# In the Mamba scan, the state product moves ahead of the next group's decay matrix, and the gated norm's steps move to other places in the queues

## What is computed

```python
cb = einsum("blgn,bsgn->blsg", cc, bc)
xdt = xc * dtc[..., None]
y_diag = einsum("blsg,blsgr,bsgrp->blgrp", cb, decay, xdt)
y_off = einsum("blgn,bgrpn->blgrp", cc, state) * exp(acs)[..., None]
decay_to_end = exp(acs[:, -1:] - acs)
new_state = state * exp(acs[:, -1]) + einsum("bsgn,bsgr,bsgrp->bgrpn", bc, decay_to_end, xdt)
...
g = (y * silu(z)).reshape(b, s, SSM_GROUPS, NORM_GROUP)
g = g * rsqrt(mean(g * g, axis=-1, keepdims=True) + EPS)
g = g.reshape(b, s, D_INNER) * norm_w
return g @ w_out
```

## Time and profile before

| What | Value |
|---|---|
| Median of three runs | 1325.86 us (1325.69 to 1330.2) |
| Profiled execution, its own time | 1325.86 us |
| Its span | 1324.1 us |
| TensorE busy | 1287.5 us, 97% of the span |
| VectorE, ScalarE, GpSimd busy | 771.0, 674.5, 143.5 us |
| Mean granted clock of TensorE | 0.998 |

### The profile page before, as it was taken

The page is one execution under the profiler, slowest core; times in us unless marked ns, Lnnn a source line. Parts: engine busy times, 40 slices in busy tenths (PEclk is TensorE's granted clock), DMA queues, the critical chain, the costliest instruction groups (busy, mean ns, idle before and its releaser), DMA issues.

```text
span 1324.1 us, 18273 instructions
## 1 busy us (share of the span) xinstructions
PE 1287.5 (97%) x6912; PEld 1097.7 (83%) x6912; DVE 771.0 (58%) x924; ACT 674.5 (51%) x886; POOL 143.5 (11%) x208
## 2 busy tenths in 40 slices
PE   7999999999989999999999999899999999999997
PEld 6888889998778888888888888687888887998895
DVE  5655645778876555554555545866555544766563
ACT  6544446665774544443544435853645535443652
POOL 3000001019940000000000002610000000000000
PEclk9999999999999999999999999999999999999999
DMA  9655645543236455564655553322655563766401
GB/s 294 201 182 188 223 131 191 173 147 96 96 123 231 155 190 190 189 198 153 191 190 190 197 192 117 138 61 89 217 181 181 182 222 99 201 181 221 154 7 48
DMA packets 180045, 218.76 MB, mean 165 GB/s; under 512 B 8617, under 2 KB 132846, under 8 KB 179982
## 3 DMA queue, kind: packets, MB, share of 16 engines
q1 hardware_dynamic: 178606, 216.70, 50.2%
q10 hardware_dynamic: 1088, 1.05, 0.2%
q0 software_dynamic: 288, 0.15, 0.1%
HBM read 216.82 MB, written 1.05 MB: 165 GB/s over the span
## 4 chain that ended last, share of the span: by engine, by line
PE 86%; DVE 5%; ACT 4%; POOL 3%; issue 1%; DMA 0%; POOLq 0%; DVEq 0%; ACTq 0%; SPq 0%
PE acc L580 27%; PE acc L582 26%; PE acc L581 26%; PE tr L597 4%; DVE w_lo L1785 2%; POOL R_hi L2456 1%; ACT w_hi L1237 1%; POOL R_lo L2456 1%; PE aux L992 1%; ACT xT_hi L1250 1%; PE acc L973 1%; POOL xdt L2465 1%; POOL ys L2468 1%; DVE xT_lo L1810 0%; PE tr L854 0%
## 5 line engine op out<-in xcount | busy, mean ns | idle before, releaser
L1785 DVE TENSOR_TENSOR w_lo<-raw,w_hi 128x2048 fp32r<-128x2048 f32 (+1 forms) x196 | 442.4, 2284 | 186.3 <-ACT w_hi L1237 186.1
L1237 ACT ACTIVATE w_hi<-raw 128x2048 fp32r<-128x2048 f32 (+1 forms) x198 | 369.5, 1900 | 117.2 <-PE acc L582 116.5
L580 PE MATMUL acc<-w_hi,xT_hi 128*128 128x512 f32 (+1 forms) x914 | 362.6, 397 | 6.5 <-DVE w_lo L2368 2.9
L582 PE MATMUL acc<-w_hi,xT_lo 128*128 128x512 f32 (+1 forms) x914 | 355.4, 389 | 0.0
L581 PE MATMUL acc<-w_lo,xT_hi 128*128 128x512 f32 (+1 forms) x914 | 354.8, 388 | 0.0
L580 PEld LDWEIGHTS acc<-w_hi,xT_hi 128*128 128x128 f32 x914 | 172.1, 188 | 42.2 <-issue 3.4
L582 PEld LDWEIGHTS acc<-w_hi,xT_lo 128*128 128x128 f32 x914 | 172.0, 188 | 36.3
L581 PEld LDWEIGHTS acc<-w_lo,xT_hi 128*128 128x128 f32 x914 | 172.4, 189 | 33.3
L580 PE MATMUL acc<-w_hi,hT_hi 128*128 128x512 f32 x448 | 175.8, 392 | 0.3 <-DVE y_sb L2278 0.3
L582 PE MATMUL acc<-w_hi,hT_lo 128*128 128x512 f32 x448 | 174.5, 389 | 0.0
L581 PE MATMUL acc<-w_lo,hT_hi 128*128 128x512 f32 x448 | 174.3, 389 | 0.0
(11 more groups left out here) (292 smaller groups left out, 1145.7 us busy)
## 6 DMA issues: line engine op xcount, KB each, us to landing
raw<-in_ffn_w_down SPq DMA_DIRECT2D x88, 512.0 KB, 4.9
raw<-in_ffn_w_gate SPq DMA_DIRECT2D x87, 512.0 KB, 4.5
raw<-in_ffn_w_up SPq DMA_DIRECT2D x87, 512.0 KB, 5.5
raw<-in_ssm_w_in SPq DMA_DIRECT2D x48, 512.0 KB, 4.5
raw<-in_w_in_a SPq DMA_DIRECT2D x64, 256.0 KB, 4.1
raw<-in_ssm_w_out SPq DMA_DIRECT2D x16, 512.0 KB, 4.0
raw<-in_mla_w_out SPq DMA_DIRECT2D x8, 512.0 KB, 4.4
raw<-in_w_out_a SPq DMA_DIRECT2D x8, 512.0 KB, 4.7
```

Source lines behind the costliest of these rows:

```text
L580: pe.matmul(o, lh, rh, start=start, stop=False, skip_group_check=skip)
L582: return pe.matmul(o, ll, rh, start=False, stop=stop, skip_group_check=skip)
L1237: inst = act.activation(w_hi[:, u % RING, 0:n], raw[:, u % RING, 0:n], ACT.Copy)
L1785: inst = dve.tensor_tensor(w_lo[:, u % RING, 0:n], raw[:, u % RING, 0:n], w_hi[:, u % RING, 0:n].bitcast(F32), ALU.subtract)
```

## The change

The task `state` is gone as a task of its own. TensorE's `y` now issues the state product right behind the 16 matmuls of y, ahead of `seg`; ScalarE copies the state under `y`, ahead of the exponentials. GpSimd's `xdtd` no longer waits for the state product of the group before. The norm's steps are moved out of `small`:

| Work | Before | After |
|---|---|---|
| gate(0), (1), (2) on VectorE | in small(16), (17), (19) | behind small(16), (18), (20) |
| gate(3) | in small(21), behind its off | behind scale_gated(2) |
| scale_gated(0), (1) | in small(18), (20), behind y | behind small(18), (20) |
| scale_gated(3) | ahead of small(22) | behind the splits of O3 and O4, ahead of small(23) |
| square_gated(1), (2), (3) on ScalarE | behind the split at the end of s = 8, 9, 10 | behind first_tap of s = 9, 10, and behind the loop |
| gated_norm(0), (1), (2) on GpSimd | behind small(17), (18), (20) | behind small(17), (19), (21) |

```diff
-MAMBA_TURNS = {"dt": 1, "acs": 1, "btok": 1, "xs": TB, "cb": 1, "y": 2, "seg": 0, "state": 0, "g": TB}
+MAMBA_TURNS = {"dt": 1, "acs": 1, "btok": 1, "xs": TB, "cb": 1, "y": 2, "seg": 0, "g": TB}
...
-    for name, first in (("y", 13), ("seg", 12), ("state", 13)):
+    for name, first in (("y", 13), ("seg", 12)):
...
                             last.then_inc(turned, 1)
+                            claim_turn(k + 1)
+                            pe.wait_ge(xdtd_ready, g + 1)
+                            pe.matmul(tr[:, (k + 1) % 2, 0:GW], Btok[:, g, :], xdtd[:], start=True, stop=True)\
+                                .then_inc(turned, 1)
                             state_turn[g] = k + 1
                             c.turn += 2
-                        elif name == "state":
-                            k = state_turn[g]
-                            claim_turn(k)
-                            pe.wait_ge(xdtd_ready, g + 1)
-                            pe.matmul(tr[:, k % 2, 0:GW], Btok[:, g, :], xdtd[:], start=True, stop=True)\
-                                .then_inc(turned, 1)
...
-                        elif name == "state":
-                            act.wait_ge(turned, k)
-                            inst = act.activation(state[:], tr[:, (k - 1) % 2, 0:GW], ACT.Copy)
-                            turn_free(inst, k - 1)
+                        elif name == "y":
+                            act.wait_ge(turned, k + 2)
+                            inst = act.activation(state[:], tr[:, (k + 1) % 2, 0:GW], ACT.Copy)
+                            turn_free(inst, k + 1)
...
                     first_tap(s)
-                    if s == 8:
-                        square_gated(0)
+                    if s >= 8:
+                        square_gated(s - 8)
                     small(2 * s + 1)
                     split_to(u0 + 2 * s + 4)
-                    if s >= 8:
-                        square_gated(s - 7)
+                square_gated(3)
...
-                            if g == G + 1:
-                                gate(3)
...
-                            if n == 18:
-                                scale_gated(0)
-                            elif n in (16, 17, 19):
-                                gate((n - 15) // 2 if n > 16 else 0)
-                            elif n == 20:
-                                scale_gated(1)
...
                     small(2 * s)
+                    if s >= 9:
+                        scale_gated(s - 9)
+                    if s >= 8:
+                        gate(s - 8)
                     split_to(u0 + 2 * s + (4 if s < 6 else 3))
...
                 scale_gated(2)
+                gate(3)
                 c.unit, c.pair = u0 + 22, p0 + 11
                 u = c.unit
                 split_to(u + 3)
-                scale_gated(3)
                 small(22)
                 split_to(u + 5)
+                scale_gated(3)
                 small(23)
...
                             pool.wait_ge(exp_done, 2 * g + 1)
-                            if g:
-                                pool.wait_ge(turned, y_turn[g - 1] + 2)
-                            y_turn[g] = k
...
-                    if n in (17, 18, 20):
-                        gated_norm((n - 16) // 2)
+                    if n in (17, 19, 21):
+                        gated_norm((n - 17) // 2)
                 gated_norm(3)
```

More of the change, by code:

```diff
@@ L2484, in gated_norm @@
                                        ALU.pow).then_inc(z_rstd, 1)
-                xs_turn, y_turn = {}, {}
+                xs_turn = {}
                 for n in range(22):
                     small(n)
-                    if n in (17, 18, 20):
-                        gated_norm((n - 16) // 2)
+                    if n in (17, 19, 21):
+                        gated_norm((n - 17) // 2)
                 gated_norm(3)
```

## The result

| | Before | After |
|---|---|---|
| Median, same chip, six runs each | 1326.77 us (1325.69 to 1330.20) | 1334.72 us (1334.00 to 1338.45) |
| Profiled execution, and its span | 1325.86, 1324.1 us | 1335.3, 1333.5 us |
| Mean granted clock in the profiled execution | 0.998 | 0.995 |

The ratio is 1.0062, 95% interval 1.0050 to 1.0075: some 8 us slower, where +3.4 us was forecast. The six executions of before are rather quick ones: over all its executions on record its median is 1328.0 us (76 of them), that of the changed kernel 1335.1 us (23), and the difference 7.0 us. The time lies outside the range given (1323.5 to 1332.5 us), and by the bound of 0.5% it is slower, the side that had the chance 0.12.

What follows compares the result with a forecast made beforehand. TensorE was taken as the bound, its gaps set by GpSimd's chain until 377 us, then by VectorE's queue. Tail +4.6 and y(7) -1.2 gave +3.4 us: 1325.9 + 3.4 = 1329.3 us, range 1323.5 to 1332.5.

Steps and rivals of the forecast that it cites:

- Part three, steps 16 to 19: Gates, scales and squares moved on VectorE at steps 16 to 19: covered by idle time, counted as nothing.
- part one: State product ahead of seg: effects taken as cancelling, shift 0 at the end of step 18, bounds -0.9 and +0.5.
- part two: norm(1) behind R(7) on GpSimd, steps 19 and 20: y(7) starts 1.2 us sooner, bounds 0.6 and 1.8.
- Part three, the tail: From y(7) to the out-projection's unit O3: uncovered gates, scales and squares delay VectorE and ScalarE, +4.6 us.
- the first rival: At the tail, VectorE catches up during O0 to O2 and no wait forms: 1324.7 or 1323.3 us, chance 0.18.
- The tail wait doesn't form: VectorE catches up during O0 to O2, TensorE keeps the 1.2 us: 1324.7 or 1323.3 us, chance 0.18.
- The clock falls as well: Waits at pairs 2 and 3 lower TensorE's granted clock, 1.7 us lost: 1331.0 us, chance 0.10.
- The table load comes onto GpSimd's chain: At steps 14, 16, 17 and 19 the load delays xdtd, up to 5.1 us: 1334.4 us, chance 0.10.
- The sum's far end: Slow bound: y(7) 0.6 sooner, chain of steps 16 and 17 +0.5, tail +5.2: +5.1 us, 1331.0 us.

Runs made afterwards that it cites:

- e4: The changed kernel with y(6) computed three times at step 19, 32 more matmuls to fill TensorE's wait: 1333.88 us, ratio 1.0050.
- e8: The changed kernel with scale_gated(0) alone moved from behind small(18) to behind small(19) on VectorE: 1331.20 us, ratio 1.0024.
- e11: The changed kernel with GpSimd writing R(7) for one head of four only, for timing alone: 1330.38 us, ratio 1.0020.
- e1: The kernel before with only the state product and its copy moved ahead of seg and GpSimd's wait removed: 1326.81 us, ratio 0.9994.
- e6: The kernel before with GpSimd's gated_norm(1) moved from behind small(18) to behind small(19): 1325.23 us, ratio 0.9985.
- e3: The changed kernel with gate(0), (1), (2) and scale_gated(0) put back into VectorE's small(16), (17), (19) and (18): 1330.23 us, ratio 1.0020.
- e5: The changed kernel with scale_gated(3) put back ahead of small(22): 1333.63 us, ratio 1.0039.
- e10: The changed kernel with scale_gated(0) behind small(19) and scale_gated(3) ahead of small(22): 1330.28 us, ratio 1.0020.
- e7: The kernel before with scale_gated(3) alone moved behind the splits of O3 and O4: 1327.63 us, ratio 0.9998.

## Why the prediction was wrong, point by point

**Part three, steps 16 to 19: the step that failed.** It read: "At steps 16 to 19 they have cover: VectorE is idle 9.3 of 44 us there and each w_lo is some 3 us ahead of need, so I count nothing". Three things were wrong in it. First, the deadline: w_lo had slack, but behind w_lo stand off and cbm, which since part one hold the bank that TensorE's next product needs, with seg queued behind that. Part one saw this new wait for step 17 ("push back by some 0.6 us") and never asked it for step 19. Second, the price: "uncovered, a gate is 1.3 us" is the row without GpSimd, as 1.13 us is for a scale; scale_gated(0) and gate(1) cost 3.41 and 2.97 us in GpSimd's regime. The kernel before already showed it, with its own gate(1) at 2.37 us beside R(7):

```profile
368.02 2.37 DVE L2041 TENSOR_TENSOR ys<-ys,sz 128x512 f32<-128x512 f32 x2
```

The lock between the two engines stood in part two, and there was charged to GpSimd alone. Third, idle time as a mean over 44 us says nothing of a queue's order at one place. Measured: +3.63 us from step 19 to Y in place of a win of 1.2, of it +1.24 us of wait, and the rest the clock behind it (2.4 us left over; 2.7 by e4). e8 (one call moved: 3.5 to 5 us back) and e11 (GpSimd shortened: 4.3 to 5.6 us back) show both conditions.

**Part one: "I take these as cancelling".** True of the state part alone (e1: 0.9994, its profiled execution +0.51 us from y(0) to step 19). In the pair this stretch lost 1.06 us, beyond the bound of +0.5. The wait of 0.64 us at step 16 is the state part's own, behind a w_lo of 3.12 us, and e1 has it too; the one of 1.81 us at step 17 isn't in e1, and there gate(0) (2.97 us) and w_lo (3.12 us) lie ahead of cbm.

**Part two: y(7) 1.2 us sooner.** The number is right where VectorE is left alone, 1.35 us from step 19 to Y in e6, but what was to limit it is not. The forecast let y(7) start when xdt(7) was ready. In e6 xdt(7) is ready at 373.74 us and y(7) starts at 376.61, with no wait ahead of it: TensorE itself sets that start, and what it won is the 1.19 us of its wait for R(7). Within the changed kernel norm(1) doesn't even wait its turn; its squares come late (gms at 372.49, idle 3.23 us), since they follow gate(1).

**Part three, the tail: right.** +4.27 us for +4.6. w_lo of O0 was forecast to start at Y+9.2 and started at 391.64 - 382.70 = Y+8.9; turns of pair 2 Y+19.65, measured Y+19.8; scale_gated(3) started at Y+32.6 (forecast Y+32.9). Its rows:

```profile
391.64 2.28 DVE L1782 TENSOR_TENSOR w_lo<-raw,w_hi 128x2048 fp32r<-128x2048 f32 x1
...
402.34 1.28 DVE L2030 TENSOR_TENSOR ys<-ys,sz 128x512 f32<-128x512 f32 x2
...
406.66 2.29 DVE L1782 TENSOR_TENSOR w_lo<-raw,w_hi 128x2048 fp32r<-128x2048 f32 x1 [3.04 <-ACT w_hi L1235]
...
415.34 1.14 DVE L2037 TENSOR_SCALAR ys<-ys,grs 128x256 f32<-128x256 f32 x4
```

The 3.04 us of idle time ahead of 406.66 is the chain gate(3), squares, w_hi that spoke against the first rival.

**The rivals.** "The tail wait doesn't form" is out. "The clock falls as well" came true in kind, but I had placed it in the tail and priced it at 1.7 us; the profile has it at step 19, at 2.7 us. "The table load comes onto GpSimd's chain" gave nearly the measured time, 1334.4 us, for a wrong reason. Its load is there, and it does delay E:

```profile
373.99 0.38 ACT L1407 ACTIVATE state<-tr 128x256 f32<-128x256 f32 x1 [1.59 <-PE tr L860]
374.39 1.28 ACT L1403 ACT_TABLE_LOAD   x1
...
375.76 1.08 ACT L1404 ACTIVATE E<-aux 128x512 f32<-128x512 f32 x2
```

but GpSimd waited for E only 2.4 us in all, in three places, and e1 and e3, which keep the load in that place, take 11.86 and 11.55 us from step 19 to Y against 12.24 before. That the number agreed is chance.

**The range.** The sum's far end was +5.1 us. It took every term singly; the case in which part one's new wait and part three's longer queue meet had no term.

## What to carry to other kernels

When a change puts a wait on a PSUM bank ahead of other work, list everything that stands in the emptying engine's queue before the instruction that frees it, after all parts of the change are in; two edits can cost far more together than one by one. Price VectorE instructions in a stretch where GpSimd never rests by a row from beside GpSimd, not by a row from a quiet stretch, and split such work off the path (one call moved by a step was worth 3.5 to 5 us). Time a change of several parts in its parts: here one small part was worth keeping.

## What the hardware showed that I had not expected

**Short VectorE instructions beside GpSimd.** Four `tensor_scalar` of 128x256 take 1.13 us alone, 2.13 us beside GpSimd instructions of 0.94, 0.66, 0.44 and 0.45 us, and 3.41 us beside those of 0.94, 0.66, 1.08 and 1.09 us; two `tensor_tensor` of 128x512 take 1.29 us alone, 1.69 us in e11 and 2.97 us in the changed kernel. Beside the `tensor_scalar` VectorE pays and GpSimd hardly; beside the gates an R instruction of GpSimd goes from 1.03 to 1.49 us, and beside one long w_lo it is GpSimd that pays most (2.66 us for 0.61).

**The clock falls in changing places.** Behind waits of TensorE of 1.8 to 3.1 us the granted clock fell in some executions and not in others of the same queue: at step 19 in the profile of after, at step 17 in those of e4 and e8, at both in e5, at pair 2 in e3 and e10, and at step 19 in e7, whose wait of 1.89 us left the clock at 1.00 in the kernel before. One fall at step 19 cost 2.7 us (e4 against after, and e7 against before); one at step 17 cost 1.5 to 1.6 us from y(0) to step 19 (66.5 us in e4, e5 and e8 for 64.9 in the changed kernel). The mean granted clock of all executions of a kernel says the rest: 76 executions of the kernel before lie mostly at 0.996 (53 of them, mean time 1328.1 us), nine at 0.998 (1326.0 us); of 23 of the changed kernel 15 lie at 0.995 (1335.1 us) and four at 0.992 (1338.4 us); of e10 six of 11 are at 0.996, and e11 spreads from 0.995 to 0.998. So the profiled execution of before, at 0.998, was one without a fall. At the same clock of 0.995 (five executions of before) the two kernels differ by 1335.1 - 1330.3 = 4.8 us; the remaining 2 to 3 us of the result (7 or 8 us in all) are my estimate for the clock. What decides in which execution a wait is followed by a fall, these runs don't tell. The Trainium skill (TensorE: Matmul & The Clock Gate, "What's actually happening") says that the chip's watch on the engine's activity runs on its own time and doesn't start with the kernel, so that the point of a change shifts from run to run; that fits these rows, and no run here tests it.
